# The second gate's projection in four quarters between the groups of the state scan

## The chip, the cores and the metric

The kernel runs on one core of a Trainium2 chip. Its time is the device time of one launch in microseconds; the figure compared is the median of several runs. Engines in the views: PE is TensorE (PEld its weight loads), DVE VectorE, ACT ScalarE, POOL GpSimd (here it only issues gathers), SP SyncE (here it only issues the other transfers).

## What is computed

One layer of a streaming encoder, for one prompt of 256 tokens and 8 streams of 16 new tokens, all in float32. Cut to what matters here:

```
proj = x @ w_in                       # q k v, indexer, z (2048), xBC (3072), dt, two gates (1024 each)
attn = sparse attention(q, k, v)      # top-k keys by an indexer
y    = ssd(conv(xBC), dt, ...)        # Mamba-2 scan, 4 groups of 8 heads
y    = rms_norm_per_group(y * silu(z))
ya, ym = attn @ w_attn_br, y @ w_ssm_br
g_a, g_m = sigmoid(gate_pre + b_gate)         # the two gates
h    = LN1(alpha * x + (g_a * ya + g_m * ym) @ w_out)
out  = LN2(alpha * h + PEER(h))       # 8 heads x 16 experts per token, rows gathered from two tables of 16384 x 1024
```

The second gate, g_m, is needed only where `ym` is there, at the end of the mixer.

## The kernel before

The 384 tokens are three tiles of 128, one pass each, in the order streams, first half of the prompt, second half (`TILE = (2, 0, 1)`). A pass is the mixer (projections, attention, scan, branch products, first norm) and the choice of experts. The experts of a tile run as a loop of 64 blocks of two expert columns (192 blocks in all), beside the next pass's mixer. A step of it is a tick: DVE makes two dot products of the hidden row with gathered rows of u (L1411), ACT a Gelu and the two scaled diagonals, TensorE adds the rows of v (L588, 16 records). POOL issues two gathers of u and two of v per block (L551), 0.5 MB each, three blocks ahead; the u gathers wait for the dots three blocks back, the v gathers for TensorE's products three blocks back. The gathers of a tile's first blocks wait for its indices (`idx_ready`, counted in quarters of a tile).

Where ticks stand in a pass is written out by hand: every engine calls `step(place)` at places with the same names, `TICKS_AT` gives the ticks of each visit in turn, (1,) where a place isn't named, and all engines must have visited the same places. `steps.limit` holds the count at 64 per pass until the next tile's first indices are made; ticks beyond are dropped, not put off.

The order of a pass, on TensorE: convolution channels, dt, q/k/v (two wide tiles), then in passes two and three z (two wide tiles) and the gates (two wide tiles, place "gates"), the turned tails of the convolution (pass three only), the turned keys (`attention`), indexer scores, selection and four items of attention, `ya`, the scan (`ssd`: sums, turned channels, then per group g the decays of g + 1, place "seg", products L970 and L975, place "y"), the turned y, `ym`, the output product, the first norm, and the experts' query. A wide tile (`wide_tile`, L658) is 1024 columns in two PSUM banks, with four weight pieces of 1 MB; fp32 matmuls show as two records each, so it has 32 records. `gate_bias` (L638) puts the bias into the bank first. Pass one handles z and the gates in another way (`fill`), with no ticks beside it.

Weights stream through a ring of four buffers of 1 MB. SP issues each piece (L430) when its buffer's last reader has signalled (`half_used`, or the signal of the filled bank); the pieces' order on SP is the order of their use. After the gates' pieces come those of `w_attn_br`, the stores of the new rows, and the first half of `w_ssm_br`.

PSUM: banks 0 to 3 are drained by DVE (`vbank`), 4 and 5 by ACT (`sbank`), 6 and 7 hold the experts' sums. ACT keeps the gates' pre-activations in GX. While the second gate tile is projected, ACT does the time steps (`time_steps`, L1073 is the line of all its activations): Exp, Ln, and the Silu over the convolution's output. Later, within the attention, one Sigmoid over all of GX. In the scan DVE makes, per group: decays (L1647 to L1657), the masked product L1670, y (L1690 to L1714). DVE multiplies `ym` with the second half of GX at L1732.

## Time and profile before

| | us |
|---|---|
| median of 3 runs | 1827.51 |
| lowest, highest | 1819.58, 1834.67 |
| the profiled execution | 1833.91 (span 1831.9) |
| PE busy | 1465.8 (80%) |
| DVE busy | 1090.7 (60%) |
| POOL busy | 807.8 (44%) |
| ACT busy | 460.1 (25%) |
| transfers | 625.16 MB, mean 341 GB/s |

Pass one ends near 459 us, pass two near 934, pass three near 1470; behind it only the experts of the last tile run. Times are from the start of the span. A row of a timeline gives start, duration, engine, line and operation, the number of records merged in it, and in brackets the idle time ahead with what ended it. A row of the view by windows gives a stretch and each engine's busy time in it, the granted clock of TensorE (1.00 is full), and the rate of the transfers.

### The profile page before, as it was taken

How to read it: one execution, taken by the hardware profiler on the slowest of the kernel's cores; microseconds unless marked ns; L12 is line 12 of the kernel's file. 1: busy time of each engine (PE TensorE's matmuls, PEld its weight loads, DVE VectorE, ACT ScalarE, POOL GpSimd, SP SyncE). 2: the span in 40 equal slices, each digit the busy share in tenths (PEclk: the TensorE clock that was granted, in tenths of full speed). 3: DMA queues.
4: the chain of work that ended last, by engine and by line, in shares of the span. 5: the costliest groups of instructions: out<-in, count | busy, mean ns of one | idle time of the engine just before them, and what ended most of it. 6: DMA issues, size and time to landing. Idle time of an engine off the chain costs nothing.

```text
span 1831.9 us, 20809 instructions
## 1 busy us (share of the span) xinstructions
PE 1465.8 (80%) x7541; PEld 697.0 (38%) x7541; DVE 1090.7 (60%) x2812; ACT 460.1 (25%) x1107; POOL 807.8 (44%) x776
## 2 busy tenths in 40 slices
PE   8989989878998877869889989688779864555564
PEld 8544566336733332433347433234333321111111
DVE  3403278237668474872587783874943699865554
ACT  1121423102210443340222113453230222221111
POOL 0000000004642476663466422775643467777773
PEclk9988888989999988879999999788879987667767
DMA  8984356659999999999999999999889999999996
GB/s 286 330 262 149 125 153 179 234 192 362 408 409 409 391 409 409 352 337 358 372 409 408 409 409 374 346 378 372 315 311 393 375 352 381 386 411 409 409 409 266
DMA packets 212949, 625.16 MB, mean 341 GB/s; under 512 B 17748, under 2 KB 55828, under 8 KB 212664
## 3 DMA queue, kind: packets, MB, share of 16 engines
q0 software_dynamic: 110736, 402.88, 57.0%
q1 hardware_dynamic: 102112, 220.96, 33.4%
q8 instruction: 60, 0.98, 0.2%
q14 instruction: 41, 0.34, 0.0%
HBM read 611.55 MB, written 12.23 MB: 341 GB/s over the span
## 4 chain that ended last, share of the span: by engine, by line
PE 46%; DMA 17%; DVE 16%; POOL 11%; issue 5%; ACT 4%; SPq 1%; DVEq 0%; ACTq 0%
PE bank L658 17%; POOL BIG L551 11%; PE bank L588 9%; PE bank L631 8%; DMA BIG<-in_peer_v_dram,BIG 7%; DMA BIG<-in_peer_u_dram,BIG 5%; DMA wbuf<-in_w_in_dram 5%; DVE BIG L1411 5%; PE bank L724 4%; PE bank L698 3%; ACT BIG L1073 2%; DVE BIG L1654 1%; DVE BIG L1682 1%; PE bank L953 1%; PE bank L638 1%
## 5 line engine op out<-in xcount | busy, mean ns | idle before, releaser
L551 POOL DMA_INDIRECT BIG<-in_peer_u_dram,BIG x384 | 396.2, 1032 | 587.0 <-DVEq L1809 428.9
L588 PE MATMUL bank<-BIG 64*64 64x512 f32 x3072 | 477.9, 741 | 211.5 <-DMA BIG<-in_peer_v_dram,BIG 126.5
L551 POOL DMA_INDIRECT BIG<-in_peer_v_dram,BIG x384 | 408.7, 1064 | 413.9 <-PE bank L588 330.9
L1411 DVE CUSTOM_DVE_ANT_0 BIG<-BIG 128x1024 f32<-128x1024 f32 x384 | 461.8, 1223 | 178.4 <-DMA BIG<-in_peer_u_dram,BIG 175.0
L658 PE MATMUL bank<-wbuf,BIG 128*128 128x512 f32 x832 | 382.1, 614 | 15.0 <-DMA wbuf<-in_w_in_dram 6.9
L588 PEld LDWEIGHTS bank<-BIG 64*64 64x64 f32 x3072 | 112.1, 155 | 528.4 <-issue 309.0
L658 PEld LDWEIGHTS bank<-wbuf,BIG 128*128 128x128 f32 x832 | 158.2, 196 | 235.7 <-issue 208.0
L1073 ACT ACTIVATE BIG<-bank 128x512 f32<-128x512 f32 (+5 forms) x231 | 117.6, 538 | 463.6 <-PE bank L698 143.6
L1073 ACT ACTIVATE BIG<-cst,small 128x64 f32<-128x64 f32 x384 | 112.0, 339 | 399.3 <-DVE small L1406 399.0
L631 PE MATMUL bank<-wbuf,BIG 128*128 128x512 f32 x320 | 153.6, 638 | 9.0 <-DMA wbuf<-in_w_in_dram 8.5
L1073 ACT ACTIVATE small<-small 128x2 f32<-128x2 f32 (+1 forms) x204 | 41.4, 204 | 410.1 <-DVE small L1411 399.1
L724 PE MATMUL bank<-BIG,wbuf 128*128 128x128 f32 x1152 | 137.4, 283 | 8.3 <-ACT BIG L1073 4.8
L724 PEld LDWEIGHTS bank<-BIG,wbuf 128*128 128x128 f32 x1152 | 134.8, 198 | 17.3 <-issue 12.0
L698 PE MATMUL bank<-cst,BIG 128*128 128x128 f32 (+3 forms) x531 | 92.0, 325 | 57.1 <-DVE BIG L1381 19.6
L1073 ACT ACT_TABLE_LOAD x97 | 124.5, 1283 | 2.5 <-PEq L1854 0.8
L698 PEld LDWEIGHTS bank<-cst,BIG 128*128 128x128 f32 (+3 forms) x531 | 69.5, 163 | 99.6 <-issue 24.4
L631 PEld LDWEIGHTS bank<-wbuf,BIG 128*128 128x128 f32 x320 | 63.9, 205 | 94.5 <-issue 88.5
L1406 DVE TENSOR_TENSOR small<-small,BIG 128x2 f32<-128x2 f32 x192 | 30.5, 159 | 84.1 <-ACT small L1073 69.8
L1732 DVE TENSOR_TENSOR BIG<-bank,BIG 128x512 f32<-128x512 f32 x6 | 4.1, 691 | 88.6 <-PE bank L658 88.6
L1423 DVE SCALAR_TENSOR_TENSOR BIG<-BIG,rowsT 128x128 f32<-128x128 f32 x144 | 50.6, 352 | 5.1
L1766 DVE FIND_INDEX8 BIG<-BIG 128x8 uint32<-128x128 f32 (+1 forms) x144 | 45.7, 329 | 0.0
L970 PE MATMUL bank<-BIG 128*128 128x64 f32 x192 | 30.6, 327 | 18.3 <-DVE BIG L1670 13.2
(163 smaller groups left out, 1043.0 us busy)
## 6 DMA issues: line engine op xcount, KB each, us to landing
wbuf<-in_w_in_dram SPq DMA_DIRECT2D x108, 1024.0 KB, 11.2
wbuf<-in_w_ssm_br_dram SPq DMA_DIRECT2D x24, 1024.0 KB, 7.6
wbuf<-in_peer_wq_dram SPq DMA_DIRECT2D x24, 1024.0 KB, 8.0
wbuf<-in_w_attn_br_dram SPq DMA_DIRECT2D x12, 1024.0 KB, 8.7
wbuf<-in_w_out_dram SPq DMA_DIRECT2D x12, 1024.0 KB, 7.8
BIG<-in_state_ssm_dram SPq DMA_DIRECT2D x16, 512.0 KB, 6.1
out_s_ssm_dram<-BIG SPq DMA_DIRECT2D x16, 512.0 KB, 3.6
BIG<-in_peer_u_dram,BIG POOLq DMA_INDIRECT x384, 7.9
```

Source lines behind the costliest of these rows:

```text
L551: pool.indirect_dma_start(slot, None, table, bass.IndirectOffsetOnAxis(ap=eidx[:, col:col + 1], axis=0)).then_inc(done, 16)
L588: last = mm(acc[i][64 * half:64 * half + 64, :], dg[rows, :], vslot[k][rows, 512 * half:512 * half + 512], start=False, stop=False, skip_g ...
L631: last = mm(dst[:, :], lhs[:, HALF * h + k, :], w[:, k, :], start=(first and h + k == 0), stop=(end and h == 1 and k == HALF - 1))
L658: last = mm(dsts[c][:, :], lhs[:, 2 * h + k, :], w[:, k, 512 * c:512 * c + 512], start=(first and bias is None and h + k == 0), stop=(end ...
L698: return nc.tensor.transpose(dst, src, ids)
L724: last = mm(dsts[c][:, j * P:(j + 1) * P], w[:, k, (4 * c + j) * P:(4 * c + j + 1) * P], xT[:, 2 * h + k, :], start=(h + k + j == 0), stop ...
L970: last = mm(dst[:, r * HD:(r + 1) * HD], q.MT[g % 2][:, r, :], q.xdt[g % 2][:, r * HD:(r + 1) * HD], start=True, stop=True)
L1073: return nc.scalar.activation(o, i, func, **kw)
L1406: tt(w8[(k - 1) % 2], gl[(k - 1) % 2], gate[:, at:at + WB], ALU.mult).then_inc(w_ready, 1)
L1411: nc.vector.tensor_tensor_reduce(uslot[s], uslot[s], H[k // BLOCKS], 1.0, 0.0, ALU.mult, ALU.add, dots[k % 2][:, j:j + 1]).then_inc(dot_do ...
L1423: own(stt(res, row[k], wr[:, 24 + k:25 + k], res, ALU.mult, ALU.add))
L1766: own(nc.vector.max_index(idx[:, at], val[:, at], s))
```

## The change

In passes two and three the projection of the second gate (the fourth of the wide tiles for z and the gates) is no longer done ahead of the attention. Its four pieces become four quarters (`gate_quarter`), one in each group of the scan, ahead of the wait for `seg_ready`; both its banks stay open from the first to the last. ACT applies the Sigmoid straight from PSUM in the last group (`glu_gate_m`), and its earlier Sigmoid covers only the first gate. SP issues the four pieces behind the stores of the new rows and ahead of `w_ssm_br`. DVE waits for ACT's reads ahead of the product with `ym`. The place "gates" is visited twice instead of four times (one tick less ahead of the attention), and "y" has two ticks at each visit instead of two and one in turn (two more in the scan).

```diff
-TICKS_AT = dict(dt=(0,), z=(1, 0), gates=(1, 0), xbt=(2,), y=(2, 1), late=(2, 1), last=(2,))
+TICKS_AT = dict(dt=(0,), z=(1, 0), gates=(1, 0), xbt=(2,), y=(2, 2), late=(2, 1), last=(2,))
@@ counts of PSUM banks
-            ssd_s = 5 + (33 if s else 4 * (t == 1))
+            ssd_s = 5 + (33 if s else 2 + 4 * (t == 1))
-                               ("z", 0, 8 * (not q.first)), ("tails", 0, 6 * (t != 0)),
+                               ("z", 0, 6 * (not q.first)), ("tails", 0, 6 * (t != 0)),
@@ SP
-                for j in range(0 if q.first else 4):
+                for j in range(0 if q.first else 3):
                     load_wide(w_in, O_Z + 1024 * j if j < 2 else O_GATE + 1024 * (j - 2), (sb_filled, at["z"][1] + 2 * j + 2))
                 load_wide(a["w_attn_br"][0], 0, (vb_filled, at["ya"][0] + 2))
                 if not q.first:
                     store_new_rows(q)
+                    load_wide(w_in, O_GATE + 1024, (sb_filled, before[n, "ssd"][1] + 7))
@@ TensorE
-                    for j in range(4):
+                    for j in range(3):
                         place = "z" if j < 2 else "gates"
+                gate_m = []
+
+                def gate_quarter(h):
+
+                    w = weights(wide)
+                    for c in range(2):
+                        if h == 0:
+                            gate_m.append(sbank(c))
+                            gate_bias(gate_m[c], 2 + c)
+                        for k in range(2):
+                            last = mm(gate_m[c][:, :], xT[:, 2 * h + k, :], w[:, k, 512 * c:512 * c + 512],
+                                      start=False, stop=(h == 3 and k == 1))
+                        if h == 3:
+                            sf.give(last)
+                    if h < 3:
+                        last.then_inc(half_used, 1)
+
                 decays(0)
                 for g in range(G):
                     if g + 1 < G:
                         decays(g + 1)
+                    if not q.first:
+                        gate_quarter(g)
                     pe.wait_ge(seg_ready, q.n * G + g + 1)
@@ ACT
                 def glu_gates():
-                    f(GX, GX, ACT.Sigmoid).then_inc(gates_ready, 1)
+                    c = slice(0, 2 * D if q.first else D)
+                    f(GX[:, c], GX[:, c], ACT.Sigmoid).then_inc(gates_ready, 1)
+
+                def glu_gate_m():
+                    for half in range(2):
+                        src = bank()
+                        sd.give(f(GX[:, D + half * 512:D + half * 512 + 512], src[:, :], ACT.Sigmoid))
-                    for i in range(4):
+                    for i in range(3):
                         step("z" if i < 2 else "gates")
@@ ACT, in the scan, behind "seg"
+                    if g == G - 1 and not q.first:
+                        glu_gate_m()
                     step("y")
@@ DVE
                 if not q.first:
-                    for _ in range(3):
-                        step("gates")
+                    step("gates")
                 step("dt")
@@
                 step("ym")
+                if not q.first:
+                    dve.wait_ge(sb_drained, SR + before[q.n, "ssd"][1] + 7)
```

## Rows read from the trace of the kernel before

**Rows 1.** Page, queues: packets, MB, share of 16 engines.
```profile
q0 software_dynamic: 110736, 402.88, 57.0%
```

**Rows 2.** View by windows: passes, end of the projections, attention, scan, one scan group.
```profile
459.00:934.30 475.30, 404.38 (x1952) 184.33 (x1945) 298.87 (x780) 133.79 (x322) 247.52 (x233) 0.90 1.00 386
934.30:1470.30 536.00, 453.64 (x2284) 216.77 (x2283) 350.34 (x891) 154.96 (x359) 273.77 (x256) 0.91 0.98 373
1470.30:1831.90 361.60, 206.95 (x1111) 47.55 (x1109) 238.24 (x567) 72.97 (x222) 261.09 (x258) 0.73 0.97 379
...
600.80:619.10 18.30, 18.30 (x57) 6.94 (x56) 6.67 (x20) 10.23 (x12) 4.05 (x4) 1.00 0.98 364
620.00:724.00 104.00, 75.86 (x454) 29.54 (x450) 68.82 (x158) 44.69 (x119) 75.87 (x76) 0.85 1.03 409
734.00:811.00 77.00, 59.64 (x359) 30.79 (x358) 63.10 (x136) 29.14 (x57) 55.59 (x50) 0.80 0.97 354
...
1144.00:1243.00 99.00, 71.95 (x420) 29.85 (x416) 74.20 (x150) 45.53 (x110) 74.90 (x72) 0.81 0.97 364
1263.00:1351.00 88.00, 63.84 (x384) 33.83 (x384) 71.52 (x149) 32.96 (x64) 58.42 (x52) 0.84 0.91 323
...
754.60:771.20 16.60, 14.12 (x84) 7.05 (x84) 15.41 (x34) 5.27 (x11) 12.05 (x13) 0.79 0.96 336
```

**Rows 3.** Timeline of POOL at the second gate; DVE's dots up to 1470.2 us.
```profile
1470.36 0.94 POOL L551 DMA_INDIRECT BIG<-in_peer_u_dram,BIG  x1 [8.50 <-DVEq L1809]
...
L1411 DVE CUSTOM_DVE_ANT_0 BIG<-BIG 128x1024 f32<-128x1024 f32 x254 | 304.3, 1222 | 85.2 <-DMA BIG<-in_peer_u_dram,BIG 84.0
```

**Rows 4.** Timeline of TensorE, pass two: first and last row around the second gate's tile.
```profile
600.75 1.12 PE L638 MATMUL bank<-BIG,cst 4*128 4x512 f32 x2
...
619.06 1.95 PE L588 MATMUL bank<-BIG 64*64 64x512 f32 x16
```

**Rows 5.** Timeline of ACT, pass two: Silu, Gelu, the keys' copies; last y tick.
```profile
605.85 2.77 ACT L1073 ACTIVATE BIG<-BIG 128x3072 f32<-128x3072 f32 x1
...
610.41 0.20 ACT L1073 ACTIVATE small<-small 128x2 f32<-128x2 f32 x1
...
622.06 0.75 ACT L1073 ACTIVATE BIG<-bank 64x512 f32<-64x512 f32 x2 [1.73 <-PE bank L799]
...
808.75 0.59 ACT L1073 ACTIVATE BIG<-cst,small 128x64 f32<-128x64 f32 x2 [7.17 <-DVE small L1406]
```

**Rows 6.** Timeline of ACT, pass three: Silu, a pair of tails, the keys' copies.
```profile
1121.52 2.76 ACT L1073 ACTIVATE BIG<-BIG 128x3072 f32<-128x3072 f32 x1
...
1136.12 1.06 ACT L1073 ACTIVATE BIG<-bank 3x512 f32<-3x512 f32 x2 [0.23 <-PE bank L698]
...
1141.57 0.75 ACT L1073 ACTIVATE BIG<-bank 64x512 f32<-64x512 f32 x2 [1.74 <-PE bank L799]
```

**Rows 7.** Timeline of SP, pass two; page, transfers by issue: count, KB, us to landing.
```profile
606.78 12.74 SPq L430 DMA_DIRECT2D wbuf<-in_w_attn_br_dram  x4
...
wbuf<-in_w_in_dram SPq DMA_DIRECT2D x108, 1024.0 KB, 11.2
```

**Rows 8.** Timeline of DVE in the scan of pass two: two ticks, two masked products.
```profile
764.77 0.16 DVE L1406 TENSOR_TENSOR small<-small,BIG 128x2 f32<-128x2 f32 x1 [0.27 <-ACT small L1073]
...
767.49 0.16 DVE L1406 TENSOR_TENSOR small<-small,BIG 128x2 f32<-128x2 f32 x1 [0.27 <-ACT small L1073]
...
769.86 1.30 DVE L1670 TENSOR_TENSOR BIG<-BIG 128x1024 f32<-128x1024 f32 x1
...
783.38 1.30 DVE L1670 TENSOR_TENSOR BIG<-BIG 128x1024 f32<-128x1024 f32 x1
```

**Rows 9.** Timeline of TensorE: L970 at both clocks, a tick after a long wait.
```profile
800.96 3.68 PE L970 MATMUL bank<-BIG 128*128 128x64 f32 x16 [3.61 <-DVE BIG L1670]
...
1302.99 1.97 PE L970 MATMUL bank<-BIG 128*128 128x64 f32 x16
...
1160.75 3.69 PE L588 MATMUL bank<-BIG 64*64 64x512 f32 x16 [6.32 <-ACT BIG L1073]
```

## What I expect of the change

> **What bounds the kernel now.** I read the page first, then stretches in the view by windows, then the timelines of single engines. One tick (one step of the expert loop, for one block) has four gathers; the software queue moved 402.88 MB for 192 ticks [rows 1], so a tick is 2.10 MB. A piece of weights is 1.05 MB, the four of a wide tile 4.19 MB. The highest rate in the windows is 409 GB/s [rows 2]; at that rate a tick takes 5.1 us and a wide tile's weights 10.2 us.
>
> Two gates cut the kernel: the gathers of blocks 64 and 128 need indices that DVE finds at the end of passes two and three. The second was issued at 1470.36 us, after 8.50 us in which POOL waited for nothing but the indices (L1809), with 254 dots made, 127 ticks of 128 [rows 3]. From there to the end are 361.6 us at 379 GB/s [rows 2], of which 64 ticks of 5.1 us are 328: transfers, which the change leaves alone. What it can win is the time of the gates. Up to the first, at 934.3, pass two runs at 386 GB/s, and from there pass three at 373 [rows 2], so at 409 there would be about 27 and 47 us to spare (475.3 x 23/409, 536.0 x 36/409). No pass can win more than that.
>
> Inside a pass the owner changes. At the end of the projections TensorE is full and transfers are not (18.30 of 18.30 us, 364 GB/s). The attention runs at 409 GB/s in pass two and at 364 in pass three. In the scan the rate is 354 and 323 GB/s, and DVE is busy 63.10 of 77 and 71.52 of 88 us [rows 2].
>
> **The change, term by term.** The times below are those of the profiled run (1833.91 us, span 1831.9). The median of the runs is 6.4 us less; differences are carried over to it as they are.
>
> 1. Front. The fourth wide tile runs from 600.75 to 619.06 [rows 4]: 18.3 us of TensorE, namely 2.1 of bias, 14.1 of products and a tick of 1.9. But this tile is cover. Beside it ACT does the time steps, three table loads, Exp, Ln and a Silu of 2.77 us that ends at 608.6; the scale of the diagonals, a table load and the Gelu follow, to 610.6 [rows 5]. The attention's first step needs ACT's two copies of the turned keys, now from 622.06 to 622.8. With the tile gone TensorE would be there some 4 us after 600.75, but ACT's copies come behind the Gelu, at 611.4. That is 11.4 us earlier, not 18.3; 7 us turn into a new wait of TensorE for ACT. In pass three the Silu ends at 1124.3, six copies of the tails follow (a pair takes 1.06 us and 0.23 ahead of it, so 3.9), then the same 2.8 us: 1131.0 against 1142.3, 11.3 us [rows 6].
>
> Transfers allow more. What leaves the front is 4.19 + 2.10 MB, 15.4 us. The attention branch's weights are asked for as the last projection tile frees its pieces, from 606.78 over 12.7 us [rows 7]; at least half of them land inside the attention, and will have landed before it. In pass two, where transfers set the attention, that gives up to 15.4 + 2.0 - 11.4 = 6.0 us more (2.0 is the idle share of the 18.3 us at 364). I take 3, of 0 to 6; in pass three, at 364 GB/s, 1 of 0 to 4.
>
> 2. Scan, DVE. The y places take two ticks each instead of 2, 1, 2, 1: two ticks more. One takes 2.72 us on DVE (764.77 to 767.49), with 0.27 the only wait; a group with two ticks takes 13.5 us (L1670, 769.86 to 783.38), so one with three 16.3 [rows 8]. That is +5.4 us in each pass.
>
> 3. Scan, TensorE. A quarter is 8 of the tile's 32 records, 3.5 us at the full clock, the first with 2.1 us of bias ahead. In the three-tick group of 16.60 us TensorE was busy 14.12, at a granted 0.79 of the clock [rows 2]; at the full clock L970 and L975, three ticks and the decays are 11.1, and 14.6 with the quarter, under 16.3. The first quarter, 5.6 us with its bias, makes L970 3.7 us late; by DVE's order, which reads it 5 us behind L1670, about 1.2 us of that is left. The last group gains: L970 took 3.68 us after 3.61 us idle, and at 1302.99, with no idle ahead, 1.97 [rows 9]: the levels of 1.2 and 2.4 GHz. The quarter fills that idle time. It is worth 1.7 us there and 1.0 on L975 behind it, nothing if the clock stays low; I take -2 of 0 to -2.7. The clock also bears on the front: the tick at 1160.75, after 6.32 us idle, took 3.69 us instead of 1.9 [rows 9], so the new wait of 7 us may cost up to the 1.8 us of one tick at half the clock in each pass. I count that in the range only.
>
> The Trainium skill ("TensorE: Matmul & The Clock Gate", section "Why this matters for your kernels") says that idle gaps between bursts drop the clock to half; the rows agree. By that rule the scan gains its full 2.7 us, and the front loses its 1.8, twice: the sum would be -15 instead of -17.
>
> 4. Scan, transfers. It gains 2 x 2.10 + 4.19 = 8.4 MB, 20.5 us. It has 77 x 55/409 = 10.4 us to spare in pass two and 88 x 86/409 = 18.5 in pass three, and grows by 4.6 us anyway. So pass two is 5.5 us short, and pass three even. Gathers run three ticks ahead, and today's scan waits for none, so part of the shortage can be made good behind it: +2.5 of 0 to 5.5 in pass two, 0 of 0 to 2 in pass three.
>
> 5. Behind the gates. The expert loop is held at tick 64 and 128. At the gates it will stand at 64 and 128 instead of 63 and 127, and the next place, held by the limit, has one tick less. The end of each pass has the same count as before (70, 134), so no tick leaves the last stretch. What is left is one tick less of DVE (2.72 us) behind each gate: 0 to -2.7, I take -1 each.
>
> 6. At nothing: ACT's two Sigmoids from PSUM (2 x 0.6) and two table loads (2 x 1.28) are 3.8 us and lie in the 7.17 us that it is idle ahead of 808.75 [rows 5]; uncovered they would put off the last y tick by as much. On SP's queue the gate's load stands behind the row stores, long released, and the state branch's weights stand behind the gate's, each after a quarter, the last near 797; even at the 11 us of a load of w_in [rows 7] it is there by 809, and its product starts after 824. The norm's loads behind it wait for the scan's end anyway. The two PSUM banks are held through the scan, where nobody else takes them. DVE's new wait ahead of the state branch's product is released some 45 us earlier.
>
> Sum. Pass two: -11.4 - 3 + 5.4 + 1.2 - 2 + 2.5 - 1 = -8.3. Pass three: -11.3 - 1 + 5.4 + 1.2 - 2 + 0 - 1 = -8.7. Together -17: 1810.5 us at the median.
>
> **The rivals.**
> - The front gives all that the transfers allow: -17.4 and -15.3 for the first terms, and no refill term. -13.8 and -11.7, so -25.5, 1802 us. For it: 409 GB/s in the attention of pass two. Against it: 364 in that of pass three.
> - The scan becomes transfer-bound and the front gives no credit: -11.4 + 10.1 - 1 and -11.3 + 6.6 - 1, -8, 1819.5 us. For it: three ticks and a piece take 17.9 us of transfers, and the group has 16.3. Against it: the three ticks of lead.
> - TensorE becomes the scan's bound at the lower clock: 14.1 us of records as today and a quarter of 7.1 are 21.2 for 16.3, 20 us per pass, so -17 + 39 = +22, 1849.5 us. The win is gone once a group exceeds 18.4 us (8.5 us over four groups). Against it: the gaps that lowered the clock are those that the quarters fill.
> - It does nothing that counts, as later waits take it back ahead of both gates: 1827.5 us.
>
> **How the numbers follow.** The forecast 0.40 (its own range 1805 to 1816), the full front 0.23, the transfer-bound scan 0.22, TensorE's clock 0.07, nothing 0.08. 1%, 18.3 us, is about what a measurement of this kernel can tell from no change, and the forecast lies just inside. Faster by over 1%: 0.18 of the forecast's 0.40 and 0.22 of the second case, 0.40. Slower by over 1%: 0.06. Within: 0.54. The best bounds together (-17.4 - 15.3 + 13.2 - 5.4 - 5.4) are -30, the worst without the clock case (+0.7 and -2.7) near zero, so 1797 to 1826.
>
> **What would show it.** Two biases and the quarters inside the scan's groups; the keys' copies about 3 us behind the Silu in pass two and 7 in pass three, and TensorE waiting some 7 us for ACT ahead of them; L1670 rows 16.3 to 17 us apart in pass two; L970 near 2 us in the last group; about 400 GB/s in the scan of pass two; the gates at about 926 and 1453, and 361 us behind the second. It is wrong if L1670 rows stand over 18 us apart, if DVE waits for u gathers in the scan, or if the gates don't move.

## The result, and the profile after

| | before | after |
|---|---|---|
| median of 20 runs each | 1827.67 | 1820.63 |
| lowest, highest | 1817.18, 1837.0 | 1813.78, 1834.39 |
| the profiled execution (span) | 1833.91 (1831.9) | 1825.84 (1823.7) |
| PE, DVE, POOL busy | 1465.8, 1090.7, 807.8 | 1454.8, 1091.0, 811.1 |

The ratio of the two is 0.9964, with a 95% interval of 0.9947 to 0.9981: 7 us faster, where 17 were forecast. The two profiled spans differ by 8.2 us, and that difference can be followed through the trace (the stretches add up to 8.3 by rounding). In this table a landmark is the start of one row in each trace, and the last column is what a stretch gained or lost since the landmark above it.

| landmark | before | after | difference | of that, this stretch |
|---|---|---|---|---|
| bias of the first gate, pass two (PE) | 579.15 | 577.93 | -1.2 | -1.2 |
| `ya` (DVE) | 730.19 | 718.78 | -11.4 | **-10.2** |
| norm of y, behind the scan (DVE) | 813.09 | 810.62 | -2.5 | **+8.9** |
| first gate | 933.87 | 929.00 | -4.9 | -2.4 |
| q and k of pass three (DVE) | 1100.18 | 1095.51 | -4.7 | +0.2 |
| `ya` | 1259.39 | 1244.63 | -14.8 | **-10.1** |
| norm of y | 1351.36 | 1342.33 | -9.0 | **+5.7** |
| second gate | 1469.76 | 1459.85 | -9.9 | -0.9 |
| end | 1831.9 | 1823.7 | -8.2 | +1.7 |

Ahead of each scan 10 us are won, and the scan gives 9 and 6 of them back. Each trace is one execution, and not every stretch repeats equally well. thin_quarters (below) changes nothing outside the scan, and its stretches agree with those of after within 0.4 us from the first gate's bias to `ya` of pass two, in the scan of pass two and up to q and k of pass three; but from there to `ya` of pass three it takes 142.4 us against 149.1. The last stretch, from its first gather, takes 359.1 to 366.7 us in the traces of before, after and the seven kernels from early_steps to thin_quarters in the table below. So pass two can be read to one to three microseconds (small_loads, with the same front, takes 143.9 us from the gate's bias to `ya` for the 140.9 of after), the attention of pass three and the last stretch only to several.

The view by windows of after, with the columns of [rows 2]: the three passes, the attention, and the scans of passes two and three.

```profile
459.00:929.00 470.00, 395.69 (x1959) 179.47 (x1952) 300.05 (x780) 135.22 (x323) 246.86 (x233) 0.92 1.01 391
929.00:1460.00 531.00, 446.11 (x2283) 212.32 (x2283) 350.55 (x892) 157.10 (x361) 276.63 (x256) 0.92 0.98 375
1460.00:1823.70 363.70, 211.91 (x1097) 48.80 (x1095) 235.94 (x564) 72.40 (x219) 261.20 (x258) 0.72 0.96 377
611.00:713.00 102.00, 75.91 (x436) 28.56 (x428) 66.88 (x155) 42.40 (x113) 72.81 (x73) 0.82 0.99 377
722.00:810.00 88.00, 69.61 (x432) 33.34 (x428) 69.01 (x148) 35.79 (x69) 64.35 (x56) 0.96 1.00 389
1248.00:1342.00 94.00, 76.43 (x456) 37.02 (x452) 76.93 (x160) 38.23 (x74) 63.67 (x60) 0.94 0.98 374
```

Set it beside [rows 2]: the attention of pass two ran at 409 GB/s and now runs at 377, its transfers being fewer, and it is not shorter (the engines' share of time only went from 1.03 to 0.99). The scan of pass two went from 354 to 389 GB/s, at 0.96 of TensorE's clock instead of 0.80. The last stretch is 2.1 us longer, which is within the spread named above.

**The front.** TensorE's timeline of after, pass two, from the third wide tile's tick to the first work of the attention:

```profile
599.54 1.95 PE L589 MATMUL bank<-BIG 64*64 64x512 f32 x16
601.41 1.09 PE L800 MATMUL bank<-cst,BIG 128*64 128x128 f32 x8
602.34 0.38 PE L803 MATMUL bank<-cst,BIG 128*64 128x128 f32 x2
610.08 3.69 PE L589 MATMUL bank<-BIG 64*64 64x512 f32 x16 [7.36 <-ACT BIG L1093]
```

ACT's timeline of after in the same stretch (L1093 is the line of all its activations):

```profile
603.34 1.28 ACT L1093 ACT_TABLE_LOAD   x1
604.63 2.76 ACT L1093 ACTIVATE BIG<-BIG 128x3072 f32<-128x3072 f32 x1
607.30 0.57 ACT L1093 ACTIVATE BIG<-cst,small 128x64 f32<-128x64 f32 x2
607.89 1.28 ACT L1093 ACT_TABLE_LOAD   x1
609.19 0.20 ACT L1093 ACTIVATE small<-small 128x2 f32<-128x2 f32 x1
609.30 0.73 ACT L1093 ACTIVATE BIG<-bank 64x512 f32<-64x512 f32 x2
```

TensorE has turned the keys at 601.4, 19.5 us earlier than before. The copies of them start at 609.30, 12.8 us earlier than in [rows 5], behind the Silu, a table load and the Gelu. In between it waits 7.36 us, and the tick behind the wait takes 3.69 us instead of 1.95, the two levels of its clock (1.2 and 2.4 GHz).

**The scan.** DVE's timeline of after, pass two: the masked product of each group, the dots ahead of it that waited, and the reads of L990 and L995 in the first and last group.

```profile
741.92 1.22 DVE L1697 TENSOR_TENSOR BIG<-BIG 128x1024 f32<-128x1024 f32 x1
749.22 0.69 DVE L1727 TENSOR_TENSOR BIG<-BIG,bank 128x512 f32<-128x512 f32 x1 [1.65 <-PE bank L990]
750.06 0.69 DVE L1732 COPY BIG<-bank 128x512 f32<-128x512 f32 x1 [0.15 <-PE bank L995]
...
759.94 1.29 DVE L1697 TENSOR_TENSOR BIG<-BIG 128x1024 f32<-128x1024 f32 x1
...
774.49 1.23 DVE L1439 CUSTOM_DVE_ANT_0 BIG<-BIG 128x1024 f32<-128x1024 f32 x1 [0.52 <-DMA BIG<-in_peer_u_dram,BIG]
...
777.01 1.22 DVE L1697 TENSOR_TENSOR BIG<-BIG 128x1024 f32<-128x1024 f32 x1
...
792.50 1.23 DVE L1439 CUSTOM_DVE_ANT_0 BIG<-BIG 128x1024 f32<-128x1024 f32 x1 [1.54 <-DMA BIG<-in_peer_u_dram,BIG]
...
794.93 1.22 DVE L1697 TENSOR_TENSOR BIG<-BIG 128x1024 f32<-128x1024 f32 x1
798.32 0.69 DVE L1727 TENSOR_TENSOR BIG<-BIG,bank 128x512 f32<-128x512 f32 x1 [1.57 <-PE bank L990]
799.16 0.69 DVE L1732 COPY BIG<-bank 128x512 f32<-128x512 f32 x1 [0.15 <-PE bank L995]
...
806.02 1.23 DVE L1439 CUSTOM_DVE_ANT_0 BIG<-BIG 128x1024 f32<-128x1024 f32 x1 [1.91 <-DMA BIG<-in_peer_u_dram,BIG]
```

The masked products stand 18.0, 17.1 and 17.9 us apart, where a group with three ticks takes DVE 16.3 [rows 8]. The difference is the first group's wait for L990 and then, new in this scan, 0.52 + 1.54 + 1.91 = 4.0 us of waiting for gathers of u. POOL's timeline in the same stretch shows what the issue of the gathers waits for:

```profile
764.20 1.45 POOL L552 DMA_INDIRECT BIG<-in_peer_v_dram,BIG  x1 [0.30 <-issue]
765.95 0.94 POOL L552 DMA_INDIRECT BIG<-in_peer_u_dram,BIG  x1 [0.30 <-issue]
767.19 1.34 POOL L552 DMA_INDIRECT BIG<-in_peer_u_dram,BIG  x1 [0.30 <-issue]
768.83 1.64 POOL L552 DMA_INDIRECT BIG<-in_peer_v_dram,BIG  x1 [0.31 <-issue]
...
797.87 0.94 POOL L552 DMA_INDIRECT BIG<-in_peer_u_dram,BIG  x1 [0.30 <-issue]
799.12 0.94 POOL L552 DMA_INDIRECT BIG<-in_peer_v_dram,BIG  x1 [0.30 <-issue]
```

Nothing. From 764.20 to 799.12 there are 24 gathers, one behind the other, each with 0.30 us of idle time ahead (at 792.97 the view puts it down to TensorE's L589, else to "issue"): 35.9 us from the first start to the last end, 1.5 us for each. A tick needs four gathers, three ticks twelve, 18 us, about the distance of the groups. POOL shows as busy for 44% of the span, and yet here it has no time to spare: the 0.30 us ahead of each issue belong to the issue. That by itself doesn't say that the issue makes the groups long. The gathers run up to three blocks ahead of the dots, and whether a dot waits also depends on how soon the rows land; the experiments separate the two.

### The profile page after: what moved, and what is told of

It reads as the page before. It is cut to its first block, busy times and chain, and to the rows that moved or that the text cites. A ratio compares the mean times of both kernels' runs of the same rounds, so it can differ in the third digit from the quotient of the medians.

```text
span 1823.7 us, 20815 instructions
## 1 busy us (share of the span) xinstructions
PE 1454.8 (80%) x7541; PEld 688.3 (38%) x7541; DVE 1091.0 (60%) x2812; ACT 464.2 (25%) x1111; POOL 811.1 (44%) x776
## 4 chain that ended last, share of the span: by engine, by line
PE 45%; DMA 19%; DVE 16%; POOL 10%; issue 5%; ACT 4%; SPq 0%; DVEq 0%; POOLq 0%; ACTq 0%
PE bank L659 15%; POOL BIG L552 10%; DMA BIG<-in_peer_v_dram,BIG 9%; PE bank L589 9%; PE bank L632 8%; DMA BIG<-in_peer_u_dram,BIG 7%; PE bank L725 4%; DVE BIG L1439 4%; DMA wbuf<-in_w_in_dram 3%; ACT BIG L1093 3%; PE bank L699 3%; DVE BIG L1709 1%; ACT L1093 1%; PE bank L973 1%; PE bank L946 1%
## 5 line engine op out<-in xcount | busy, mean ns | idle before, releaser
L552 POOL DMA_INDIRECT BIG<-in_peer_u_dram,BIG x384 | 403.0, 1050 | 602.5 <-DVEq L1838 440.6
L589 PE MATMUL bank<-BIG 64*64 64x512 f32 x3072 | 481.0, 744 | 226.1 <-DMA BIG<-in_peer_v_dram,BIG 143.6
L659 PE MATMUL bank<-wbuf,BIG 128*128 128x512 f32 x768 | 352.1, 614 | 12.1 <-ACT BIG L1093 4.3
L589 PEld LDWEIGHTS bank<-BIG 64*64 64x64 f32 x3072 | 111.9, 153 | 545.4 <-issue 329.8
L1093 ACT ACTIVATE BIG<-bank 128x512 f32<-128x512 f32 (+5 forms) x231 | 117.2, 538 | 442.1 <-PE bank L699 144.3
L659 PEld LDWEIGHTS bank<-wbuf,BIG 128*128 128x128 f32 x768 | 146.3, 195 | 213.1 <-issue 191.6
L1093 ACT ACTIVATE BIG<-cst,small 128x64 f32<-128x64 f32 x384 | 112.1, 339 | 394.4 <-DVE small L1434 394.3
L632 PE MATMUL bank<-wbuf,BIG 128*128 128x512 f32 x320 | 154.0, 638 | 8.1 <-DMA wbuf<-in_w_in_dram 7.6
L1093 ACT ACTIVATE small<-small 128x2 f32<-128x2 f32 (+2 forms) x204 | 41.5, 205 | 422.4 <-DVE small L1439 413.0
L699 PEld LDWEIGHTS bank<-cst,BIG 128*128 128x128 f32 (+3 forms) x531 | 70.6, 165 | 109.5 <-ACT BIG L1093 30.7
L632 PEld LDWEIGHTS bank<-wbuf,BIG 128*128 128x128 f32 x320 | 63.9, 205 | 94.7 <-issue 89.5
L1093 ACT ACTIVATE BIG<-BIG 128x1024 f32<-128x1024 f32 (+3 forms) x33 | 33.5, 1015 | 36.5 <-DVEq L1841 24.4
## 6 DMA issues: line engine op xcount, KB each, us to landing
wbuf<-in_w_in_dram SPq DMA_DIRECT2D x108, 1024.0 KB, 10.1
wbuf<-in_w_attn_br_dram SPq DMA_DIRECT2D x12, 1024.0 KB, 11.3
```

Of the source, the lines that this page charges most:

```text
L552: pool.indirect_dma_start(slot, None, table, bass.IndirectOffsetOnAxis(ap=eidx[:, col:col + 1], axis=0)).then_inc(done, 16)
L589: last = mm(acc[i][64 * half:64 * half + 64, :], dg[rows, :], vslot[k][rows, 512 * half:512 * half + 512], start=False, stop=False, skip_g ...
L632: last = mm(dst[:, :], lhs[:, HALF * h + k, :], w[:, k, :], start=(first and h + k == 0), stop=(end and h == 1 and k == HALF - 1))
L659: last = mm(dsts[c][:, :], lhs[:, 2 * h + k, :], w[:, k, 512 * c:512 * c + 512], start=(first and bias is None and h + k == 0), stop=(end ...
L699: return nc.tensor.transpose(dst, src, ids)
L1093: return nc.scalar.activation(o, i, func, **kw)
```

## The experiments

The forecast had named two suspects for what could go wrong, transfers and TensorE's clock, and priced two parts, the tile and the ticks. The runs take these apart first, then look for the bound of the scan and of the attention. All ratios are against the kernel before, run on the same chip (its medians there were 1825.1 to 1828.0, so a ratio compares two kernels better than their medians do).

| kernel | median | ratio, 95% interval |
|---|---|---|
| after | 1820.63 | 0.9964 (0.9947 to 0.9981) |
| early_steps | 1807.80 | 0.9874 (0.9838 to 0.9911) |
| early_steps_before | 1829.14 | 1.0016 (0.9988 to 1.0045) |
| tile_alone | 1810.02 | 0.9900 (0.9865 to 0.9936) |
| ticks_alone | 1833.08 | 1.0037 (1.0015 to 1.0059) |
| tile_early | 1799.07 | 0.9832 (0.9790 to 0.9875) |
| small_loads | 1823.37 | 0.9976 (0.9949 to 1.0003) |
| thin_quarters | 1825.47 | 0.9986 (0.9957 to 1.0015) |
| tick_to_ym | 1800.64 | 0.9849 (0.9811 to 0.9886) |
| half_rows | 1810.86 | 0.9909 (0.9879 to 0.9940) |
| one_v | 1707.96 | 0.9341 (0.9299 to 0.9384) |
| ticks_to_product | 1807.79 | 0.9895 (0.9859 to 0.9931) |

**Was the fourth tile the cover of ACT's time steps?** In after, and in before as the control, the time steps run one wide tile earlier:

```diff
-                        if i == 2:
+                        if i == 1:
                             time_steps()
```

> The changed kernel, with ACT's time steps one wide tile earlier (behind the drain of the second z tile instead of the first gate tile), so that they lie beside the first gate tile. Lost cover (my theory): TensorE's wait of 7.4 us in pass two and 7.0 in pass three ahead of the attention's keys goes, the keys are turned some 6.5 us earlier after the last projection, and both gates move: about -11 us against the changed kernel, 1809 us, ratio to before 0.990. In pass two the transfers have about 8 us of idle share between 600 and 650 us, so they allow it. Rival, transfer-paced attention: the second half of the attention runs at 409 GB/s, so TensorE only waits later, the branch product of the attention does not move in pass two, and the total is 0 to -4 us against the changed kernel, ratio 0.994 to 0.996.

> The kernel before, with the same move of ACT's time steps. Lost cover: here nothing waits for them, the second gate tile is the cover, so 0, at most 1 us either way. Rival, time steps that cost in themselves (ACT or table loads late for someone else): a few us slower or faster, as in the changed kernel.

In before nothing changes (1.0016). In after it brings 13 us more by the medians, 16 by the ratios. TensorE's timeline of early_steps at the same place:

```profile
605.58 1.09 PE L800 MATMUL bank<-cst,BIG 128*64 128x128 f32 x8
606.50 0.38 PE L803 MATMUL bank<-cst,BIG 128*64 128x128 f32 x2
607.51 1.95 PE L589 MATMUL bank<-BIG 64*64 64x512 f32 x16 [0.62 <-ACT BIG L1093]
```

The wait of 7.36 us is 0.62, and the tick is back at 1.95 us. So this wait is what the removal of the tile had laid open, and it existed in before only as covered work. Of the 7.4 + 1.7 us that it cost at this place, `ya` of pass two gets 4.3 back (-14.5 us against -10.2, each counted from the first gate's bias); that of pass three gets 13 (-23.2 against -10.1, counted from q and k), more than its wait. Against the same stretch of small_loads and thin_quarters, whose fronts are those of after, it is 10 and 6, so most of the excess is the spread of that stretch.

**The two parts apart.** tile_alone is after with the ticks where before has them; ticks_alone is before with the ticks of after.

```diff
# tile_alone, against after
-gates=(1, 0), xbt=(2,), y=(2, 2)
+gates=(1, 1), xbt=(2,), y=(2, 1)
# ticks_alone, against before
-gates=(1, 0), xbt=(2,), y=(2, 1)
+gates=(1, 0, 0, 0), xbt=(2,), y=(2, 2)
```

> The changed kernel with its ticks where they stood: one at each of the two visits of gates, and 2, 1, 2, 1 in the scan. Only the projection moves. Theory, the moved ticks cost more in the scan (2 x 2.72 us of DVE and up to 4 us of waits for u gathers in pass two) than they give in front, where TensorE waits for ACT anyway: 6 to 8 us per pass better than the changed kernel less the third place's tick, so -18 us against before, ratio 0.990. Rival, the ticks taken out in front are what lets the attention end earlier: then this one has only the 11 us of the front less about 5 us of transfers per pass, -8 to -10 against before, ratio 0.995, no better than the changed kernel.

> The kernel before with only the ticks moved: one fewer beside the gates, two each at the four y places; the projection stays ahead of the attention. Theory, the ticks cost 5.4 us per scan (DVE) and give at most TensorE's 1.9 us in front and 1 behind the gate: +4 to +9 us, ratio 1.003. Rival, ticks are worth their 5.1 us of transfers in front: 0 to +2 us, ratio 1.000.

The tile alone gives 18 us by the ratio (12 to 25 by its interval) and the ticks alone cost 7 (0.0037 x 1825). The change is worth 7, not 11; by these intervals the missing 4 us can't be told from nothing. The traces do show them, in the scans. From `ya` to the norm of y, in us:

| | before | ticks_alone | tile_alone | after |
|---|---|---|---|---|
| scan, pass two | 82.9 | 87.6 | 82.5 | 91.8 |
| scan, pass three | 92.0 | 94.8 | 92.2 | 97.7 |

In pass two the ticks alone add 4.7 us, the tile takes 0.4 away, and both together add 8.9: 4.6 us come only when both are there (2.6 in pass three). In tile_alone the masked products stand 18.0, 13.5 and 16.8 us apart, with 0.4 us of waits for gathers of u. In ticks_alone there are three ticks in each group, as in after, and DVE waits for no gather; its masked products:

```profile
750.73 1.22 DVE L1670 TENSOR_TENSOR BIG<-BIG 128x1024 f32<-128x1024 f32 x1
766.88 1.30 DVE L1670 TENSOR_TENSOR BIG<-BIG 128x1024 f32<-128x1024 f32 x1
783.12 1.22 DVE L1670 TENSOR_TENSOR BIG<-BIG 128x1024 f32<-128x1024 f32 x1
799.27 1.29 DVE L1670 TENSOR_TENSOR BIG<-BIG 128x1024 f32<-128x1024 f32 x1
```

They stand 16.2 us apart, DVE's own time. POOL issues there without a pause too, a gather every 1.45 us (762 to 812), so twelve gathers take 17.3 us and the group 16.2, and the lead pays for the difference. Three ticks in each group are therefore not enough to make DVE wait.

**Both improvements together.** tile_early is after with the ticks of tile_alone and the time steps of early_steps.

> Both measures that helped alone: the projection moved with the ticks left in place, and ACT's time steps one wide tile earlier. The front loses 16.4 us of TensorE in each pass with no new wait. If the wait for ACT is what is left in front, pass three gives it in full (-16 to -20), and pass two gives what the transfers allow, 10.2 us of weights and 2 of idle share, -12; the scans add nothing. Sum -28 against before, 1797 us, ratio 0.985. Rival, the two measures overlap (both only let the attention begin earlier, which then waits for gathers in both passes): not faster than the better one alone, ratio 0.988 to 0.990.

1799.07 us, ratio 0.9832. It is faster than before and after, and the fastest of this study that computes the reference's values, though tick_to_ym can't be told from it. Its view by windows, the passes:

```profile
459.00:922.80 463.80, 394.73 (x1943) 178.37 (x1940) 298.71 (x776) 134.91 (x320) 248.10 (x233) 0.92 1.01 395
922.80:1438.50 515.70, 442.59 (x2284) 211.10 (x2283) 350.99 (x890) 156.20 (x361) 270.83 (x256) 0.93 1.00 388
1438.50:1801.10 362.60, 210.10 (x1111) 48.06 (x1109) 238.35 (x569) 72.98 (x222) 263.00 (x258) 0.72 0.96 378
```

All of it is ahead of the second gate: in the profiled runs -31.3 us there and -30.8 at the end, and the last stretch keeps its 362.6 us.

**Is the scan bound by the transfer of the weights, or by TensorE?** In small_loads a piece of the second gate carries 32 of 1024 columns; in thin_quarters the pieces are whole and the quarters' products are 32 columns wide.

```diff
# small_loads
-                    sp.dma_start(wide[b], source[:, 2 * h:2 * h + 2, :]).then_inc(w_in_sem[b], 16)
+                    sp.dma_start(wide[b][:, :, 0:cols], source[:, 2 * h:2 * h + 2, 0:cols]).then_inc(w_in_sem[b], 16)
# thin_quarters
-                            last = mm(gate_m[c][:, :], xT[:, 2 * h + k, :], w[:, k, 512 * c:512 * c + 512],
+                            last = mm(gate_m[c][:, 0:32], xT[:, 2 * h + k, :], w[:, k, 512 * c:512 * c + 32],
```

> The changed kernel, with the second gate's pieces of passes two and three only 32 of 1024 columns wide: the quarters multiply what the ring held before, so the second gate's values in passes two and three are not the reference's; all else is as it was. It takes 4 MB of transfers out of each pass, those that are asked for during the attention's branch product and whose successors land in the scan. Transfers short in the scan of pass two: its 4.0 us of waits for u gathers go, the L1697 rows come back from 17.1 to 18.0 us to about 16.3, about -4 us in pass two, 0 in the scan of pass three, and with the rates elsewhere -4 to -6 in all, 1815 us. Rival, TensorE or the order makes the groups longer: nothing changes in the scan's row distances.

> The changed kernel, with each of the quarters' products 32 columns wide instead of 512, so that the second gate's other columns in passes two and three are only their bias: 3 us less of TensorE in each group, the bias stays. If DVE and the gathers set the scan: row distances as in the changed kernel, the first group 0.5 to 1 us shorter, the last L970 slow again (up to 2.7 us lost), total within 3 us of the changed kernel. Rival, TensorE is the scan's bound since the change: groups 1 to 3 us shorter, 8 us or more over both passes, 1812 us.

small_loads missed. Neither kernel is faster than after. In small_loads DVE still waits 1.67 + 1.53 us for u, and the masked products stand 18.0, 18.1 and 17.9 us apart. With nearly nothing for TensorE to do in the quarters they stand 17.1, 17.9 and 17.9 apart, 3.2 us of waits for u stay, TensorE's clock in the scan is 0.83 instead of 0.96, and DVE's wait of 3.2 us for L990 in the last group is back. So it is not TensorE's work in the quarters that makes DVE wait for gathers; it raises the clock.

For the transfers small_loads is no such test: it doesn't lighten the scan. SP's rows of after, small_loads and ticks_alone, in this order, and the view by windows of the same three:

```profile
745.33 46.84 SPq L430 DMA_DIRECT2D wbuf<-in_w_ssm_br_dram  x4
745.36 47.90 SPq L430 DMA_DIRECT2D wbuf<-in_w_ssm_br_dram  x4
717.22 12.74 SPq L430 DMA_DIRECT2D wbuf<-in_w_ssm_br_dram  x4
```

```profile
742.00:808.00 66.00, 52.69 (x331) 23.74 (x330) 55.50 (x115) 23.21 (x47) 50.81 (x43) 1.00 1.01 397
742.00:808.00 66.00, 54.19 (x331) 24.25 (x330) 55.19 (x117) 23.23 (x47) 50.52 (x44) 0.97 1.00 392
742.00:808.00 66.00, 50.40 (x340) 25.54 (x332) 58.39 (x125) 22.33 (x44) 51.78 (x46) 0.87 0.97 356
```

The second gate's own pieces are issued from 708 us on, ahead of the scan, in both after and small_loads. They fill the ring of four, and each quarter frees one buffer, so that the four pieces of `w_ssm_br` come into the scan, whole in both kernels (397 and 392 GB/s, 1.01 and 1.00 of the transfers' share). In before and ticks_alone these pieces are issued ahead of the scan's first group, and the scan runs at 345 and 356 GB/s. What the change added to the scan's transfers is the state branch's weights, and no run takes them out while the quarters stay. POOL's one wait for TensorE there, 2.7 us behind the first quarter (746.62 in after), decides nothing: neither thin_quarters nor ticks_alone has it, and DVE waits for u in the first and not in the second; half_rows (below) has it, and DVE hardly waits.

**How late do the rows land?** Counted in order, the dot at 774.49 of after waits for a gather whose issue had ended 7.6 us before; the waits at 792.50 and 806.02 end 7.0 and 8.5 us behind theirs. In ticks_alone the dot at 798.12 reads rows whose issue had ended 4.6 us before, and waits for nothing. The median time from issue to landing of the v gathers is 8.3 us in after and 6.1 in ticks_alone (742 to 808).

**Bytes or issues?** half_rows is after with the gathers behind the first six of each table moving half a row; one_v makes one gather of v per block instead of two.

```diff
# half_rows
+                if col >= SLOTS:
+                    o = 512 * (col // SLOTS % 2)
+                    slot, table = slot[:, o:o + 512], table.rearrange("e (h n) -> (e h) n", h=2)
                 pool.indirect_dma_start(slot, None, table, ...)
# one_v
-                    for j in range(WB):
+                    for j in range(1):
```

> The changed kernel, with every gather behind the first six moving half a row (0.25 MB instead of 0.5) from a table seen as rows of 512, so that the experts' sums are not the reference's; POOL issues as many gathers as before, DVE and TensorE work on whole slots as before. Theory, POOL's issue paces the attention and the scan (1.28 and 1.47 us for each gather, occupied 96 of 101 and 66 of 66 us): the L1697 rows of the scan of pass two stay 17 to 18 us apart, a tick of the attention stays near 5.2 us, and even the last stretch, 256 gathers of about 1.28, stays above 310 us behind its gate; the whole gains at most 20 us, by the gathers that land sooner. Rival, transfers pace them (409 GB/s): with half the bytes the scan's groups fall to DVE's 16.3 us, the attention of pass two shortens by 20 us or more, and the last stretch by over 100 us.

> The changed kernel, with one v gather for each block instead of two, whose rows TensorE uses for both columns, so that the experts' sums are not the reference's: three issues a tick instead of four, and three quarters of the bytes. Theory, POOL's issue: the scan's groups of pass two fall from 17.1 to 18.0 to DVE's 16.3 to 16.6 us with no wait for u gathers, and the last stretch shortens by a quarter of its gathers, to about 270 us behind its gate. In the attention the ticks fall below 5 us until ACT, DVE or TensorE set the pace. All in all -80 to -110 us. Rival, neither issues nor bytes but the order of the engines within the scan makes its groups 17 to 18 us long: those distances stay.

Half the bytes of nearly every gather are worth 10 us, a quarter of the gathers left out (with their bytes, half as many as half_rows leaves out) is worth 113. The waits of POOL over 200 us of the last stretch of half_rows, 1560 to 1760, in columns of total, times and longest, with the row of the view by windows for the same stretch:

```profile
POOL BIG L555 <- issue: 34.4, 113, 0.3
POOL BIG L555 <- PE bank L592: 7.0, 23, 0.3
```

```profile
1560.00:1760.00 200.00, 117.28 (x548) 22.89 (x544) 93.49 (x177) 29.25 (x105) 158.76 (x136) 0.63 0.63 181
```

In half_rows 158.8 + 34.4 + 7.0 = 200 of 200 us of POOL are taken (the 7.0 are 23 gaps of the same 0.30 us that the view puts down to TensorE) while the transfers run at 181 GB/s, a share of 0.63. But an issue now takes 1.17 us (158.76/136) and not the 1.00 that it takes in after in the same stretch (153.36/154), so the last stretch grew from 363.7 to 389.7 us, and the kernel's 10 us are two things: 36 us won up to the second gate, and 26 lost behind it. Why the half row costs more to issue isn't known. Split by stretches, against after:

| | half_rows | one_v |
|---|---|---|
| attention, pass two | +2.2 | -11.8 |
| scan, pass two | -4.5 | -4.5 |
| attention, pass three | -6.5 | -14.5 |
| scan, pass three | -0.3 | -1.3 |
| last stretch | +26 | -59 |

(Stretches as in the first table. In pass three the attention's figures are within the spread of that stretch or not far above it. The last stretch of one_v takes 304 us where 270 were expected.)

The attention of pass two gets no shorter with half the bytes, and 12 us shorter with a quarter of the gathers left out. POOL's time explains it. In before, 623.97 to 718.25, it issues 74 gathers without a pause, one every 1.29 us; the shortest seen is 0.93 + 0.30. From the copies of the keys to `ya`, before:

```profile
POOL BIG L551 <- issue: 22.0, 72, 0.3
POOL BIG L551 <- PE bank L588: 6.9, 7, 5.1
622.00:730.20 108.20, 80.06 (x452) 30.93 (x450) 67.18 (x156) 44.36 (x117) 78.37 (x79) 0.86 1.03 410
```

78.4 + 22.0 are 100.4 of 108.2 us. In after there are 80 us without a pause, at 1.31 each. half_rows is no clean test of the bytes here, as its issues stand 1.46 us apart in this stretch, 9 us more for the same 62 gathers; it shows that POOL's issue alone can hold the attention at this length, not what the bytes would be worth with issues as short as in after. DVE's waits for u in the attention of pass two were 19.7 us in after, 26.3 in half_rows and 5.0 in one_v.

The scan of pass two is another matter. There both edits bring the second and third group to 16.2 us, DVE's own time (the first keeps its wait for L990, 18.0), and the waits for u to 0.2 and 0 us. In half_rows POOL issues the same number of gathers, without a pause and nearly as slowly (1.46 us apart against 1.48, 0.3 us for twelve), and the distances of 17 to 18 us that the theory expected did not stay: they fell to 16.2, the sign of the rival. So in the scan the bytes count, with issues alone as many as before. What half_rows won up to the second gate beyond these stretches it won mostly ahead of the first gate's bias of pass two and of q and k of pass three, 9.7 and 13.6 us. Its issues are no shorter there, so beside the projections bytes count too.

**More ticks where DVE waits anyway.** tick_to_ym moves a tick of tile_early out of the attention to `ym`; ticks_to_product takes ticks out of the scan to `ym`, where DVE has 28.6 us of idle time in tile_early.

```diff
# tick_to_ym, against tile_early
-gates=(1, 1), xbt=(2,), y=(2, 1)
+gates=(1, 1), item3=(1, 1, 1, 1, 0), ym=(2, 1), xbt=(2,), y=(2, 1)
# ticks_to_product, against tile_early
-gates=(1, 1), xbt=(2,), y=(2, 1)
+gates=(1, 1), ym=(2, 2), xbt=(2,), y=(1, 1)
```

> As the kernel with both measures, and the last tick of the attention of each pass stands in the state branch's product instead. If the attention's second half is transfer-paced (409 GB/s) and the branch product has idle transfers, this moves 2.1 MB from the one to the other: up to 5.1 us less per pass in front against 1.9 to 2.7 more at the product, -4 us in all against both measures. Rival, the pace of the attention is the engines': 0 to +4 us.

> As the kernel with both measures (the projection moved with its ticks left, the time steps earlier), with two ticks of each scan moved to the state branch's product: one at each y place and two at each of the two places of the product. POOL waits for TensorE over 11 us in that product and is occupied throughout in the scan. Theory, POOL and DVE set the scan: -5.4 us there against 2 x 1.9 to 2.7 us at the product, where TensorE is full, so 0 to -2 us per pass, ratio to before 0.981 to 0.984. Rival, the scan has other limits at 2.5 ticks a group: +4 to +8 us, ratio 0.986.

Both missed. tick_to_ym can't be told from tile_early, as its rival had it. By the medians ticks_to_product is 9 us slower than tile_early (the intervals of the ratios just overlap): it wins 4.1 us in the scan of pass two and then loses them, and more, where the ticks went. Four ticks in a row stand ahead of DVE's first read of the output product, one more than in tile_early, and DVE's timeline shows the fourth without its rows:

```profile
848.50 0.16 DVE L1434 TENSOR_TENSOR small<-small,BIG 128x2 f32<-128x2 f32 x1 [0.37 <-ACT small L1093]
853.63 1.23 DVE L1439 CUSTOM_DVE_ANT_0 BIG<-BIG 128x1024 f32<-128x1024 f32 x1 [4.98 <-DMA BIG<-in_peer_u_dram,BIG]
...
856.04 1.23 DVE L1439 CUSTOM_DVE_ANT_0 BIG<-BIG 128x1024 f32<-128x1024 f32 x1 [1.18 <-DMA BIG<-in_peer_u_dram,BIG]
```

It is not the issue that comes too slowly there. POOL waits 7.9 us for TensorE's products, until 840.17, and issues these two gathers of u at 842.67 and 843.91 (counted in order); their rows are used 10 and 11 us behind the end of the issue, in a stretch (837 to 857) in which the transfers run at 408 GB/s, the output product's weights among them.

## Why the prediction was right and wrong

The direction was right and the size was not, 7 us for 17. 1820.6 lies outside the forecast's own range of 1805 to 1816 and inside the widest one of 1797 to 1826. The step that failed is the credit of 3 and 1 us in step 1; smaller shares come from the scan and from behind the gates.

- **Step 1, ACT's chain: right.** For pass two 11.4 us were forecast. The copies of the keys came 12.8 us earlier, 1.2 of which were there ahead of the gates: 11.6. The wait of 7 us was 7.36 and 7.03. early_steps shows that it is the loss of cover, by taking it away. In pass three the copies came 14.2 us earlier instead of 11.3 (from where q and k stood), as the Silu came 3.9 us sooner than I had set it.
- **Step 1, the credit of 3 and 1 us: wrong.** "In pass two, where transfers set the attention" is the step that failed. It rested on 409 GB/s. Relieved of the weights, the attention ran at 377 and took as long, 109.5 us from the keys' copies to `ya` for 108.1. POOL has no time to spare there: one gather every 1.29 us without a pause for 94 us in before, 80 us at 1.31 in after. Weights that leave the front give it no time. 12 us went with a quarter of the gathers in one_v, none with half the bytes in half_rows (whose issues are longer). Instead of a credit, pass two lost 1.4 us of what the copies had won; that is about the tick at half the clock, which the text had in its range and not in its sum, and no more than this stretch varies. Its front won 10.2 us in after, 9.9 in thin_quarters and 7.1 in small_loads, against 14.4 forecast. In pass three 4.1 were lost, with DVE's waits for u in the attention up from 13.8 to 20.1 us; but that stretch gained 10.1 us in after, 13.5 in small_loads and 16.8 in thin_quarters against the 12.3 forecast, so for pass three the traces don't tell whether the credit was there.
- **Step 2, two ticks at 2.72 us: right.** In pass three the second masked product stands 18.4 us from the next, and stood 15.7: +2.7. Alone, the ticks add 4.7 and 2.8 us to the scans and cost the kernel 7, not 10.8. One tick fewer ahead of the attention is in the 7 as well; the rest wasn't separated.
- **Step 3, the quarter on TensorE: right, in the main.** L990 of the last group takes 2.00 us, where the same records (L970) took 3.68 in before [rows 9], and in pass two DVE waits 1.57 + 0.15 for it and L995 instead of 3.2 + 1.1, 2.6 us of gain for the 2 forecast; in pass three the last group gained 1.0 (it grew by 1.7 with a tick of 2.7 more). The first quarter was sized 1.2 us and cost 1.5 and 1.3. The Trainium skill ("TensorE: Matmul & The Clock Gate", section "Why this matters for your kernels") says of idle gaps between bursts that they halve the clock, and this trace agrees in both places: 3.69 us for the tick behind the new gap, 2.00 for L990 where a gap of 3.61 us was filled down to 2.56. thin_quarters puts the gap back, and the wait with it.
- **Step 4, the shortage: mechanism right as far as the runs show, size 4.0 for 2.5.** The sum took 2.5 and 0 us of 0 to 5.5 and 0 to 2; DVE's waits for u were 4.0 in pass two. The transfers of the scan rose to 397 GB/s at 1.01 of their share (742 to 808). The waits are gone where the same ticks meet fewer bytes: in half_rows, and in ticks_alone, where the state branch's weights land ahead of the scan. They stay in small_loads and thin_quarters, which leave those weights in the scan. What step 4 left out is POOL: twelve gathers take it 17.3 to 17.7 us against a group of 16.3, so it uses up the lead from which the shortage was to be made good. In before, 742 to 808, its 50.2 us of busy time and 11.9 of "issue" are already 62 of the 66 us. In all the scans grew by 8.9 and 5.7 us for 7.1 and 4.6.
- **Step 5, a tick less behind each gate: wrong.** -1 each was taken of 0 to -2.7; +0.2 and +1.7 came. Behind the second gate POOL's issues pace the experts, as the last stretch of half_rows shows, so DVE's part of a tick gives nothing; the 1.7 us are within the spread of that stretch.
- **Step 6, at nothing: right.** ACT's Sigmoid of the second gate is one row of 1.09 us at 796.57, and the last group's next tick (801.23) waits for nothing. The norm's chain has the same 1.88 us of wait as before. What was missing here is the time between scan and gate: -2.4 and -0.9 us, where I had nothing.

By stretches, measured less forecast: front +4.2 and +2.2, scans +1.8 and +1.1, behind the scans -2.4 and -0.9, behind the gates +1.2 and +2.7, ahead of it all -1.2: +8.7, which takes -17 to -8.3, the difference of the profiled runs.

The rival that gave -8 us (the scan bound by transfers, no credit in front) had the time, 1819.5, and most of the mechanism: no credit in the front of pass two, scans longer by 10.1 and 6.6 us where 8.9 and 5.7 were measured, and 17.9 us of transfers for three ticks and a piece of weights, near the 17.1 and 17.9 us of the later groups of pass two. What it lacks is POOL, which uses up the lead of three ticks that spoke against it. That its time agrees to 1 us is partly luck: in the profiled runs the front won 1 us less in each pass than it said, and the stretches around the gates gave and took some. The third rival, TensorE at the lower clock, falls with the 0.96.

Open remains how the scan's 4 us divide between POOL, which uses up the lead, and the late landing of the rows: without the bytes (half_rows, ticks_alone) the lead lasts through four groups at nearly the same rate of issue, and without a quarter of the gathers (one_v) it isn't used up. A run with the quarters in place and the state branch's weights loaded elsewhere would settle whether those weights alone make the rows late.

## What to carry to other kernels

Before a block of TensorE work is moved, look at what the other engines do beside it: here 7 of a tile's 18 us turned into a wait for ACT, and starting that work one tile sooner, worth nothing before the move, was worth 13 us after it. Look too at which transfers the move pushes along in a shared ring: here the state branch's weights, and not the moved ones, came into the scan. Before a stretch is called transfer-bound because its rate is at the highest seen, add up the issuing engine's busy time and its "issue" gaps; if they fill the stretch without a pause, issues count whatever the bytes do. But an engine that issues without a pause need not delay anybody yet: the lead and the time to landing decide that, so look for a run with the same issues and fewer bytes before the bytes are dismissed. A unit of background work needs its issue time (four gathers, 5 to 6 us) at every place where it stands, however idle the engine that consumes it is.

## What the runs showed of the hardware

- A gather of 128 rows of 4 KB takes POOL 0.93 to 2.0 us to issue (all but three in after), with 0.30 us more between two: 1.3 us each in the last stretch of after and 1.5 in its scan. 0.524 MB in 1.28 us are 409 GB/s, the same figure that I had read as the limit of the transfers. In the last stretch one can't tell the two apart by the rate.
- The issue of half a row is not cheaper: 1.17 us in the last stretch (1560 to 1760) for 1.00 in after, and 1.10 for 1.15 in the scan of pass two.
- From the end of a gather's issue to the use of its rows 7.0 to 8.5 us passed where DVE waited for them in the scan of after (1.01 of the transfers' share); 4.6 us were enough in ticks_alone (0.97). In ticks_to_product it was 10 and 11 us behind a wait of POOL for TensorE, at 408 GB/s.
- A table load is 1.28 us on ACT here, and the next activation starts at its end (607.89 + 1.28, then 609.19).
- TensorE's clock in the scan of pass two rose from 0.80 to 0.96 with quarters of dense products in its gaps, and the same records (L970 in before, L990 in after) took 2.00 us instead of 3.68 in the last group.
